# A two-layer encoder with sliding and dilated attention: the third Q/K/V projection split by token stream into two passes over its weights

## The reference, cut to what matters

```
h = rms_norm(x)
qa, ka, va, qb, kb, vb = split(h @ w_in)                 # 1024 -> 2304
oa = banded_attention(rope(qa), rope(ka), va, 128)       # stage A: 8 heads, 2 key heads
ob = dilated_mixture(rope(qb), rope(kb), vb)             # stages B0, B1: 4 heads of 64 each
x = x + concat(rms_norm(oa), rms_norm(ob)) @ w_out
x = x + cross_attention(rms_norm(x), mem)                # stage X
x = x + conv_ffn(rms_norm(x))
```

## Time and profile before

| | us |
|---|---|
| median of 3 runs | 2278.42 (2276.42 to 2281.46) |
| the profiled execution's own time | 2279.74 |
| its span | 2277.9 |
| mean granted clock of TensorE | 0.989 of full |
| first layer: scores of B0 from / of B1 from / output projection from | 199.8 / 289.7 / 318.0 |
| second layer: the same | 1323.1 / 1413.1 / 1444.7 |

### The profile page before, as it was taken

The page is one execution under the profiler, slowest core; times in us unless marked ns, Lnnn a source line. Parts: engine busy times, 40 slices in busy tenths (PEclk is TensorE's granted clock), DMA queues, the critical chain, the costliest instruction groups (busy, mean ns, idle before and its releaser), DMA issues. The chain is left out here.

```text
span 2277.9 us, 36510 instructions
## 1 busy us (share of the span) xinstructions
PE 2184.5 (96%) x13528; PEld 1920.3 (84%) x13528; DVE 1096.9 (48%) x2157; ACT 630.9 (28%) x1562; POOL 937.9 (41%) x1090
## 2 busy tenths in 40 slices
PE   7999989999999999999999999999999999999997
PEld 7989977887888888888898988789878888888885
DVE  3575655436554145225356665554364532451352
ACT  3455354234211011001044554433342100110012
POOL 3312203452455456555442122135334554555554
PEclk9999989999999999999999999899999999999998
DMA  5200111220122221222241000122111211122212
GB/s 218 69 20 29 38 66 66 74 74 29 48 65 65 65 65 55 66 64 64 65 148 38 29 29 29 65 84 75 56 38 57 65 65 57 64 64 65 65 57 91
DMA packets 41988, 144.86 MB, mean 64 GB/s; under 512 B 4880, under 2 KB 5136, under 8 KB 41616
## 3 DMA queue, kind: packets, MB, share of 16 engines
q1 hardware_dynamic: 34560, 119.02, 16.5%
q10 hardware_dynamic: 7312, 24.21, 3.0%
HBM read 133.78 MB, written 9.44 MB: 63 GB/s over the span
## 5 line engine op out<-in xcount | busy, mean ns | idle before, releaser
L752 POOL CAST w_hi<-w_landed_tile 128x1024 fp32r<-128x1024 f32 x216 | 224.8, 1041 | 1302.5 <-PE ps L802 1290.2
L756 POOL TENSOR_TENSOR w_lo<-w_landed_tile,w_hi 128x256 fp32r<-128x256 f32 x864 | 705.4, 846 | 17.3
L802 PE MATMUL ps<-x_turned,w_hi 128*128 128x512 f32 (+1 forms) x3072 | 666.8, 339 | 3.7 <-DVE regions L1474 1.9
L802 PEld LDWEIGHTS ps<-x_turned,w_hi 128*128 128x128 f32 x3072 | 523.1, 188 | 106.5 <-issue 5.4
L802 PE MATMUL ps<-w_hi,x_turned 128*128 128x256 f32 (+1 forms) x2304 | 541.8, 318 | 13.2 <-ACT scratch L1228 6.8
L802 PEld LDWEIGHTS ps<-w_hi,x_turned 128*128 128x128 f32 x2304 | 387.0, 191 | 38.0 <-issue 9.3
L802 PE MATMUL ps<-x_turned,w_lo 128*128 128x512 f32 (+1 forms) x1536 | 394.3, 338 | 0.0
L802 PE MATMUL ps<-w_hi,regions 128*128 128x512 f32 (+1 forms) x1312 | 374.7, 369 | 0.0
L802 PE MATMUL ps<-w_lo,x_turned 128*128 128x256 f32 (+1 forms) x1152 | 357.3, 310 | 0.0
L802 PEld LDWEIGHTS ps<-w_hi,regions 128*128 128x128 f32 x1312 | 238.7, 188 | 42.0 <-issue 0.7
L1278 ACT ACTIVATE scratch<-scratch 128x768 f32<-128x768 f32 x44 | 37.3, 848 | 838.2 <-DVE scratch L1544 838.2
(11 more groups left out here) (93 smaller groups left out, 2060.9 us busy)
## 6 DMA issues: line engine op xcount, KB each, us to landing
w_landed_tile<-weights_dram SPq DMA_DIRECT2D x216, 512.0 KB, 3.5
x_hbm<-x_residual ACTq DMA_DIRECT2D x2, 3072.0 KB, 13.3
x_residual<-x_hbm ACTq DMA_DIRECT2D x4, 1536.0 KB, 8.7
rows<-mem_in_dram ACTq DMA_DIRECT2D x8, 512.0 KB, 4.7
scratch<-mem_in_dram ACTq DMA_DIRECT2D x8, 512.0 KB, 6.6
x_residual<-x_in_dram SPq DMA_DIRECT2D x12, 256.0 KB, 6.3
gain<-gains_dram ACTq DMA_DIRECT2D x3, 512.0 KB, 13.3
out<-x_residual ACTq DMA_DIRECT2D x6, 256.0 KB, 3.7
```

The costliest lines, as they stand in the source:

```text
L752: nc.gpsimd.tensor_copy(W_HI[:, s, :], W_IN[:, s, :]).then_inc(w_rounded, 1)
L756: ins = nc.gpsimd.tensor_tensor(W_LO[:, s, c], W_IN[:, s, c], W_HI[:, s, c].bitcast(F32), ALU.subtract)
L802: ins = pe.matmul(dst, lhsT, rhs, start=start, stop=stop, skip_group_check=True)
```

## The change

B1's projection is made in two passes over the same weight tiles. The first does couples 0 and 1 (48 items), and stands where the whole one stood. The second, `short`, does couple 2 (24 items) and is woven, with four of the residual's transposes, over six steps from S0. The weight tiles of B1 are laid out twice, so that each layer has 114 tiles instead of 108. `outa` and what goes with it is woven over S6 to S13. The other parts of `t out 0` to `t out 3` (the short stream's) move in there too.

```diff
+SHORT_STEPS = 6
-def qkv_items(stage):
+def qkv_items(stage, couples=(0, 1, 2)):
...
-            for p in range(3):
+            for p in couples:
                 out.append([("qkv", stage, c, k, p)])
                 if k == KD - 1:
                     out[-1].append(("raw", stage, c, p))
             if pend:
                 out[-1] += pend.pop(0)
         turned = c < 2 or stage == "A"
-        pend = [[("prep", stage, c, 0)], [("prep", stage, c, 1)], [("prep", stage, c, 2)]]
+        pend = [[("prep", stage, c, p)] for p in couples] + [[]] * turned
         if turned:
-            pend[1].append(("t", "qk", stage, c, 0))
-            pend[2].append(("t", "qk", stage, c, 1))
-            pend.append([("t", "qk", stage, c, 2)])
+            for i, p in enumerate(couples):
+                pend[i + 1] = pend[i + 1] + [("t", "qk", stage, c, p)]
...
 def beside_last_stage():
-    out = [[item] for k in range(KD // 2) for item in turn_items("out", k)] + [[("unspill", 0)]]
-    late = [[("memload", b, TURNED) for b in range(3)]]
+    early = [[("t", "out", k, 0)] for k in range(KD // 2)]
+    late = [[("t", "out", k, 1)] for k in range(KD // 2)] + [[("unspill", 0)]]
+    late += [[("memload", b, TURNED) for b in range(3)]]
...
-    first, second, third = qkv_items("A"), qkv_items("B0"), qkv_items("B1")
+    first, second = qkv_items("A"), qkv_items("B0")
+    third, short = [qkv_items("B1", couples) for couples in couples_of("B1")]
...
-    items += weave(steps[b - 1:b + 2], turned)
-    items += weave(steps[b + 2:], beside)
+    c = b - 1 + SHORT_STEPS
+    items += weave(steps[b - 1:c], spread(turned, short, 2))
+    items += weave(steps[c:], beside)
...
+def qkv_bank(stage, c, p):
+    return 1 + (c + 1) % 2 if stage == "B1" and p == 2 else p
...
-                    elif i == 0:
-                        pe.wait_ge(lo_done, at(l, ("t", "qk", stage, 1, 2)))
+                    elif stage != "A" and h == 0 and t in (0, SEQ // P):
+                        pe.wait_ge(lo_done, at(l, ("t", "qk", stage, 1, keys_landed(stage, i))))
...
-        for h in range(2):
+        for h in (0, 1, 1):
             chunks += [np.arange(b0 + s * 512 + h * 256, b0 + s * 512 + h * 256 + 256) for s in range(3)]
```

More of the change, by code:

```diff
@@ L175, in qkv_items, with couples_of @@
         turned = c < 2 or stage == "A"
-        pend = [[("prep", stage, c, 0)], [("prep", stage, c, 1)], [("prep", stage, c, 2)]]
+        pend = [[("prep", stage, c, p)] for p in couples] + [[]] * turned
         if turned:
-            pend[1].append(("t", "qk", stage, c, 0))
-            pend[2].append(("t", "qk", stage, c, 1))
-            pend.append([("t", "qk", stage, c, 2)])
+            for i, p in enumerate(couples):
+                pend[i + 1] = pend[i + 1] + [("t", "qk", stage, c, p)]
     return out + pend
+def couples_of(stage):
+    return ((0, 1), (2,)) if stage == "B1" else ((0, 1, 2),)
 def sums_items(what, c):
@@ L207, in beside_last_stage @@
 def beside_last_stage():
-    out = [[item] for k in range(KD // 2) for item in turn_items("out", k)] + [[("unspill", 0)]]
-    late = [[("memload", b, TURNED) for b in range(3)]]
+    early = [[("t", "out", k, 0)] for k in range(KD // 2)]
+    late = [[("t", "out", k, 1)] for k in range(KD // 2)] + [[("unspill", 0)]]
+    late += [[("memload", b, TURNED) for b in range(3)]]
     late += [[item] for k in (KD // 2, KD // 2 + 1) for item in turn_items("out", k)]
     late += [[("scale", "mem", b)] for b in range(3)] + [[("square", "ob0", t)] for t in range(NT)]
-    return out, weave_steps(first_half_out(), late)
+    return early, weave_steps(first_half_out(), late)
 def mem_keys():
@@ L402, in banks_of @@
     if kind == "qkv" and it[3] == 0:
-        return [(it[4], ("raw", it[1], it[2], it[4]))]
+        return [(qkv_bank(it[1], it[2], it[4]), ("raw", it[1], it[2], it[4]))]
     if kind == "memk" and it[2] == 0:
@@ L613, in prep_index, with raw_of @@
         def prep_index(it):
-            return it[2] * 3 + it[3]
+            return number[("prep",) + it[1:4]]
+        def raw_of(it):
+            return raw[(number[("raw",) + it[1:4]] - 1) % 3]
         def t_bank(it):
@@ L857, in do @@
                     _, stage, c, k, p = it
-                    if k % 4 == 0 and p == 0:
+                    bank = qkv_bank(stage, c, p)
+                    if k % 4 == 0 and p in [couples[0] for couples in couples_of(stage)]:
                         begin_tile(l * TPL + tile_at[0])
@@ L865, in do @@
                         if k == 0 and t % 2 == 0:
-                            free(l, it, p)
-                        ins = acts_first(PS[:, p, (t % 2) * 256:(t % 2) * 256 + 256],
+                            free(l, it, bank)
+                        ins = acts_first(PS[:, bank, (t % 2) * 256:(t % 2) * 256 + 256],
                                          [xt[s][:, k, t * P:(t + 1) * P] for s in range(2)],
@@ L1227, in do @@
                         half = slice(256 * j, 256 * j + 256)
-                        ins = nc.scalar.activation(raw[p][:, half], PS[:, p, half], ACT.Copy,
+                        ins = nc.scalar.activation(raw_of(it)[:, half], PS[:, qkv_bank(stage, c, p), half], ACT.Copy,
                                                    scale=RS[:, 2 * p + j:2 * p + j + 1])
@@ L1235, in do @@
                         first = P if stage == "A" else 0
-                        src = raw[p].rearrange("p (j n) -> p j n", j=2)[:, :, first:256]
+                        src = raw_of(it).rearrange("p (j n) -> p j n", j=2)[:, :, first:256]
                         nc.scalar.copy(region(stage, "v")[:, 2 * p:2 * p + 2, :, HIT],
@@ L1386, in do @@
                     dve.wait_ge(raw_done, at(l, ("raw", stage, c, p)))
-                    src = raw[p].rearrange("p (j n) -> p j n", j=2)
+                    src = raw_of(it).rearrange("p (j n) -> p j n", j=2)
                     first, heads = 0, 4
```

## The result

The changed kernel takes 2308.68 us (median of 4 runs, 2307.68 to 2313.24) against 2277.42 us (2276.02 to 2281.46): ratio 1.0132, 95% interval 1.0117 to 1.0146. It is 31 us slower, four times as much as forecast (+7.5), above the forecast's own range (2281 to 2293) and above the wide one (2265 to 2298).

The account below looks back on a forecast made before the run. TensorE, busy 96% of the span, was taken to bound the kernel, so only its idle time and slow clock count. Start +1.5, tail +6.8 and B0 -0.8 gave +7.5 us: 2286 us, own range 2281 to 2293.

Parts of the forecast that it names:

- the forecast's own range: Whole kernel: 2281 to 2293 us around the predicted 2286, up to a third clock fall in each layer.
- the wide one: Whole kernel: the range for 8 in 10, 2265 to 2298 us.
- What bounds it: Whole kernel: TensorE busy 96% of the span; only its standing time and time with its clock down can change.
- the net zero of the moved work: B0 and B1: 18.2 us of products per layer move, B0 that much shorter and B1 that much longer.
- Weight tiles at nothing in S0 to S5: S0 to S5: six more weight tiles per layer loaded and split, with supply costing nothing.
- The waits in S0, S2 and S4: TensorE waits of 2.2 us in S0, 1.1 and 3.6 in S2, 4.1 in S4: 11.0 us per layer.
- The tail: S6 to S13: waits sum to 7.2 us, 1.7 each at third and fifteenth output items; net +3.4 per layer.
- the reads: S6 to S13: output items wait for banks, 2.1 us at the fifth and 1.1 at the seventeenth.
- the two waits for a bank: B0, at the two ends of a chunk: waits of 2.1 and 1.7 us behind the exponentials; stage net -0.4 per layer.
- one fall for each of the two long waits: S2 and S4: one clock fall each at 3.0 us, 6 us per layer; none at S0.
- the third rival: Clock falls also at S0, in the tail and in B0, four or five per layer: +20, 2299 us; chance 0.09.
- the three signs of being wrong: Preparations take 2 us, mean clock rises above 0.995, or S6 to S13 keep their 3.8 us idle.

Follow-up runs that it names:

- experiment 1: Changed kernel with the short pass's transposes of Q and K five items behind their preparation instead of one: 2281.04 us, ratio 1.0004.
- experiment 4: Changed kernel with POOL's split of the next tile after the short pass's preparation at chunk ends, not beside it: 2301.72 us, ratio 1.0085.
- experiment 7: experiment 5 plus later residual transposes in S0 to S3, later long-pass Q/K transposes, and output projection in whole groups of four: 2244.33 us, ratio 0.9856.
- experiment 3: Changed kernel with 26 unread products before each of the two waited-for short-pass transposes of Q and K (S2, S4): 2298.76 us, ratio 1.0081.
- experiment 8: Kernel before the change with 51 unread products per layer before five waited-for residual transposes in S0 to S2: 2264.37 us, ratio 0.9928.
- experiment 5: Changed kernel with short-pass Q/K transposes five items behind preparation and the long pass using banks 0, 1, 2 in turn: 2268.34 us, ratio 0.9959.

## Why the prediction was wrong

The sum of excess (idle time, and length times the clock's missing share) in us per layer, forecast and measured:

| | forecast | first layer | second layer |
|---|---|---|---|
| B0: waits | 3.8 | 4.4 | 4.4 |
| B0: slow clock | 0 | 3.8 | 5.4 |
| S0 to S5: waits | 11.0 | 11.3 | 11.3 |
| S0 to S5: slow clock | 6.0 | 8.3 | 8.4 |
| S6 to S13: waits | 7.2 | 8.2 | 8.2 |
| S6 to S13: slow clock | 0 | 2.0 | 2.0 |
| sum | 28.0 | 38.0 | 39.7 |

The measured ones are length minus busy, and length times one minus the clock, from the six rows of stretches above. The forecast misses by 10.0 and 11.7, 21.7 us together, and 17.9 of that is slow clock.

- What bounds it, and the net zero of the moved work: right. The measured excess of both layers, 77.7 us, less that of before, 22.1 + 26.3 with the idle time of B0 and the tail (and 4.2 and 3.7 us in the second layer), is 29.3 us, and the spans differ by 28.7.
- Weight tiles at nothing in S0 to S5: right. TensorE waits there for DVE alone; experiment 1 is level with before with all tiles in.
- The waits in S0, S2 and S4: right, mechanism and size. They were put at 2.2, 1.06, 3.6 and 4.1 us and measured 2.22, 1.08, 3.43 and 4.52. That those in S2 and S4 come from the transpose one item behind its preparation, experiment 1 shows; that the preparation is slow because of the split, experiment 4 does: 3.8 us to 2.1. (The prediction's 1.99 and 4.07 us run to the start of the next operation; to the end of the last one they are 2.08 and 4.15.) By the rule of the Trainium skill ("SBUF — State Buffer", "Who interferes with whom"), under which the later of the two instructions is blocked until the first is finished, the estimate was up to 5.0; the trace agrees in kind, with a price of 1.7 to 2.1 us for four operations.
- The tail: mechanism right, a little short. 1.7 and 1.7 for the second tile were 1.40 and 2.36, the reads 2.1 and 1.1 were 2.19 and 1.19. Experiment 7 takes the reads' waits away and leaves 2.0 us for two tiles.
- B0: the two waits for a bank right (2.1 and 1.7; measured 2.20 and 1.72), but not that the clock would stay up behind the first. So the stretch got 14.7 and 13.2 us shorter, not 18.5.
- **The step that failed**: "I take one fall for each of the two long waits ... None at S0, whose 2.2 us has items straight behind it." There were five falls per layer, not two: behind S0's 2.22 us, behind B0's 2.20 and behind the tail's 2.19 as well. The sum put the falls at 6.0 us per layer, and they measured 14.1 and 15.7. Items straight behind a wait did not protect the clock here; all three waits have them. What I had as the third rival (falls at S0, in the tail and in B0, four or five per layer) is what happened, and at 2299 it was priced too low as well, as the clock stayed down for 10.2 us in S2 (0.62 and 0.53 over two slices of 6 us), and for 6.8 and 10.2 us in B0. That these falls cost what their length says is shown from three sides: experiment 3 (the waits' ends kept, TensorE kept busy: -9.9 us), experiment 8 (-16.1 of a possible 18.5), and experiment 7, where the excess of the first layer is 5.4 us instead of 38.0 at full clock: twice 32.6 is 65.2, and 64.4 were won. All traces say the same: in the eight kernels with 13528 products TensorE's busy time, less half the length of the slow stretches (without the one at the very end, which every kernel has), is 2165.7 to 2169.4 us. So the moved work is net zero, and what sets the kernels apart is idle time and half the slow time: from before to after 17.3 and 10.2 of the 28.7 us.

The error of judgement behind it: I tied the fall to one long wait (2.83 us), set the limit just below it, and gave 2.2 us a clean clock. The rows of before already spoke against that. Their second fall, at 305.5 us, has no long wait before it: the slice 302 to 308 holds 3.85 us busy of 6, with the idle time in pieces of which the longest is 1.19 us; it is the same in the second layer, with 1.15.

```profile
303.04 0.44 PE L854 MATMUL ps<-eye,x_residual 128*128 128x128 f32 x2 [0.68 <-DVE probs_turned L1383]
303.76 0.66 PE L854 MATMUL ps<-eye,x_residual 128*128 128x128 f32 x4 [0.29 <-DVE probs_turned L1383]
305.61 0.69 PE L854 MATMUL ps<-eye,x_residual 128*128 128x128 f32 x2 [1.19 <-DVE x_turned L1378]
```

On the other side, waits of 1.64 to 1.77 us elsewhere in that trace had no fall. So the trace could not tell what 2.2 us would do, and the sum should have carried the three waits of 2.1 to 2.2 us at even odds. All three at 3 us are 9 a layer, 2304 us, beyond the range's end and nearly the result. None of the three signs of being wrong that the prediction named would have shown this either: the preparations took 3.8 us, the mean clock fell to 0.985, and S6 to S13 had 8.2 us idle.

What stays open: which of the shorter waits bring the clock down, and why one slow stretch is 3.4 us long and another 10.2 behind like waits (S2 and S4 in the changed kernel, S4 in the two layers of experiment 4, S0 in different kernels). Every trace is one execution, and the lists of falls are of that one. The tail's sizes were measured together in experiment 7 and not one by one.

## What to carry to other kernels

Filler that is itself a chain (project, scale, rotate, transpose) is only filler if its links lie apart: when a pass is narrowed from three couples to one, what stood two contraction slices behind its source stands a third of the time behind it, and has to be moved back. List the distances in time, not in items, of each product from what it waits for, before and after such a change. And price a wait of TensorE at its length and half of a slow stretch besides, with the odds that the traces show: here all 12 waits of 2.8 to 4.5 us had a slow stretch (3.4 to 10.2 us long), 31 of 34 waits of 2.19 to 2.23 us, and 4 of 14 of 2.34 to 2.37 us (all ten traces together, from 20 us on). Length alone does not tell among the shorter ones. In the changed kernel this put 10 us of slow clock on top of 17 us more of idle time.

## What the runs showed of the hardware

The same wait does and does not bring the clock down. In the changed kernel, the second wait for a bank in B0 is 1.72 us and the following 6 us run at full clock:

```profile
252.23 0.39 PE L818 MATMUL ps<-w_hi,x_turned 128*128 128x256 f32 x1 [1.72 <-ACT scratch L1245]
...
252.00:258.00 6.00, 5.77 (x51) 5.60 (x52) 5.86 (x14) 2.09 (x7) 2.18 (x3) 1.00 0.31 87
```

In experiment 1 the list is the same up to there, the wait the same to the hundredth, and the clock falls, to 0.63 over the slice behind it:

```profile
251.43 0.38 PE L819 MATMUL ps<-w_hi,x_turned 128*128 128x256 f32 x1 [1.72 <-ACT scratch L1246]
...
252.00:258.00 6.00, 6.00 (x39) 5.71 (x38) 4.85 (x13) 1.21 (x3) 1.38 (x2) 0.63 0.26 87
```

The wait in S0 shows it too: in experiment 5 it is 2.23 us in both layers, and only the second one brings the clock down (1.00 and 0.72 over the 6 us from there).

```profile
273.68 0.55 PE L873 MATMUL ps<-eye,x_residual 128*128 128x128 f32 x3 [2.23 <-DVE probs_turned L1403]
273.00:279.00 6.00, 5.32 (x44) 4.88 (x45) 3.42 (x9) 3.06 (x7) 3.86 (x5) 1.00 0.01 3
...
1391.42 0.40 PE L873 MATMUL ps<-eye,x_residual 128*128 128x128 f32 x1 [2.23 <-DVE probs_turned L1403]
1391.00:1397.00 6.00, 5.58 (x34) 5.27 (x34) 2.19 (x6) 2.35 (x6) 3.83 (x5) 0.72 0.01 3
```

So the length of such a wait doesn't settle it, and kernels that differ only elsewhere may differ by some 3 us for it. That is what experiment 1 gave back in B0 (78.4 us against 75.3). In the changed kernel a wait of 2.36 us in the tail (378.63) brought no fall either, while those of 2.19 to 2.22 us did in both layers.

Products whose results nobody reads can be worth their instructions where TensorE would stand anyway: 51 a layer, in waits of 0.7 to 2.8 us, took 0.7% off the kernel before.

Four operations of DVE with both inputs in SBUF took 2.1 us alone and 3.8 to 4.15 us beside four subtractions of POOL, and those got longer too, from 2.80 to 3.91 us.
